# Gathering whole token rows, two expert blocks to a buffer

## The chip, the cores and the metric

The kernel runs on one core of one Trainium2 chip. The metric is device time in microseconds (us) of the whole program, a two-layer model in float32. Four compute engines matter here: TensorE (PE) with its weight-load side (PEld), VectorE (DVE), ScalarE (ACT) and GpSimd (POOL). SyncE (SP) only issues transfers. All transfers, from whichever queue, run on the core's 16 DMA engines.

## The reference

The model is two blocks in a row over 512 tokens of width 1024. The change touches only the routed experts of the first block:

```
N_EXPERTS = 64; TOP_K = 8; D_EXPERT = 256; ROUTED_SCALE = 2.5
h2   = rmsnorm(x) * (1 + scale) + shift                  # [512, 1024]
# each token picks 8 of 64 experts (4 of 8 groups first), weights normalised, times 2.5
for each expert e, over the tokens that chose it:
    hid = silu(h2[tok] @ w_gate[e]) * (h2[tok] @ w_up[e])   # [n, 256]
    out[tok] += weight * (hid @ w_down[e])                  # [n, 1024]
```

Before this stage lie the first block's mixers and projections, after it the second block.

## The kernel before

All work is written out by hand per engine, with semaphores between them; `wait_ge(*x.at("step", i))` waits until step i of engine x is done. Each engine runs its own instruction list in order.

**Blocks.** The 512 x 8 routed pairs are sorted into slots, 64 slots to a block, 96 blocks. Experts are ranked by their token count. The 32 fullest have two blocks each, the other 32 have one, and `blocks` alternates between the two kinds. Slots beyond an expert's count are empty; their index lies out of bounds and the transfer skips them. What does not fit goes to an overflow loop (`ov_*`), which each engine enters before block `MID` = 48 (POOL at 47), at least once.

**The tables.** DVE turns the slot table into `GI`, indices of half rows. A token's 4 KB row of `h2` is stored as two 2 KB halves (`K.h2d2`), and partitions 0 to 63 index the first half, 64 to 127 the second. The scatter of results uses the same `GI`.

**The queue of one block**, i from 0 to 95:

- POOL, `gather(i + 6)` (line 2296): one indirect DMA of 128 half rows into `XG[i % 6]`, one block to a buffer, six buffers. Then it waits for `y(i)` from ACT and for the scatter of block i - 3 (they add into the same of three DRAM tensors `yd`), and issues `scatter(i)` (line 2322), an indirect DMA that adds 128 half rows of results. POOL enters the overflow loop just before `gather(53)`.
- PE, step i: the gate and up products of block i (line 2006, 32 matmul instructions); then `tokens_T(i + 1)` (line 2068), four 128x128 transposes of the next block's gathered rows; then the down product of block i - 1 (line 2020); then the transposition of the hidden rows of block i (line 2027).
- ACT: silu (2097); `y(i - 1)`, the weighted copy of the down product into one of four buffers `Y` (2104), which first waits for the scatter of block i - 5 out of that buffer; the copy of the transposed hidden rows (2107).
- DVE: silu times up (2279); then `tokens_dve(i + 1)` (line 2289), the copy of the transposed tokens out of PSUM into `XGT`, of which there are two, one block each.
- SP: the weights of an expert, 2 MB of gate and up (`in_w_gu`, line 1912) and 1 MB of down (`in_w_dn`, line 1915), into a ring of three, each as soon as its place is freed by the expert three before.

Before the loop, POOL issues gathers 0 to 5 and PE runs `tokens_T(0)`; `tokens_T(1)` also waits for the slot tables.

Of the kernel before, what the change touches and what calls it, by code (L numbers as in the profile page):

```python
# [1825 lines left out]
def experts(K):  # L1826
# [4 lines left out]
    S, C, I, ps = K.S, K.C, K.I, K.ps  # L1831
    H2T = K.H2T
    hi = K.area(K.base1 + 4096, K.keep1)
    XG = [hi(512) for _ in range(4)]
    ar = K.area(K.keep1)
    ar(4096)
    GUB, DNB = [], []
# [8 lines left out]
    OH, TMP = K.area(ar.at - 4096)(2048), ar(2048)  # L1846
    rows = K.area(K.R0, K.R0 + 3072)
    Y = [rows(512) for _ in range(4)]
    XGT = [rows(512).rearrange("p (c n) -> p c n", c=4) for _ in range(2)]
    later = K.area(K.base1)  # L1850
    HD, HDT = [later(128), later(128)], [later(128), later(128)]
    r256 = lambda: ar(256).rearrange("p (t n) -> p t n", t=4)
# [8 lines left out]
    ERK, NOV, EXI = ar(64), ar(1), ar(MORE)  # L1861
    SLf, SLi, Pi, Bi, Pf, Bf = (ar(32) for _ in range(6))
    E0, TB, GI, WS = (later(160) for _ in range(4))
    HS, HST = [Y[0][:, 0:256], Y[0][:, 256:512]], [Y[1][:, 0:256], Y[1][:, 256:512]]
    PSI, PSW = PP[:, :, 0, :], PP[:, :, 1, :]
    XGf = K.area(K.base1 + 4096)(2048)
# [79 lines left out]
    def pe(e):  # L1946
        K.norm2.done(e)
        e.wait_ge(*came_wr.at())
        for t in range(4):
            for k in range(8):  # L1950
                x = e.matmul(ps[5][:, t * 64:t * 64 + 64], H2T[:, k, hs(t)], wrt[:, k, :], start=(k == 0), stop=(k == 7))
        x.then_inc(*mm.up("route"))
        e.wait_ge(*came_gu[2].at(0))
        shared_gu(e, 0)
        shared_gu(e, 1)
        shared_down(e, 0)
        e.wait_ge(*dve.at("sel"))
        for t in range(4):
            for q in range(t):
                e.matmul(ps[6][:, t * 64:t * 64 + 64], C["ones"], SEL[:, q, :], start=(q == 0), stop=False)  # L1960
            x = e.matmul(ps[6][:, t * 64:t * 64 + 64], C["sup"], SEL[:, t, :], start=(t == 0), stop=True)
        for q in range(4):
            e.matmul(ps[7][:, 0:64], C["ones"], SEL[:, q, :], start=(q == 0), stop=(q == 3))
        for q in range(4):
            x = e.matmul(ps[7][0:64, 64:66], SEL[:, q, :], C["ones"][:, 0:2], start=(q == 0), stop=(q == 3))
        x.then_inc(*mm.up("counts"))
        shared_down(e, 1)
        e.wait_ge(*dve.at("H"))
        e.matmul(ps[5][:, 0:64], C["ones"][0:64, :], G1[0:64, :], start=True, stop=True)
        e.matmul(ps[5][0:2, 64:128], C["tok"][0:64, 0:1].broadcast_to([64, 2]), H[0:64, :], start=True, stop=True).then_inc(*mm.up("ranks"))  # L1970
        e.wait_ge(*dve.at("novc"))
        e.matmul(ps[7][:, 128:192], novc.broadcast_to([64, 128]), C["sup"][0:64, 0:64], start=True, stop=True)
        e.matmul(ps[7][:, 192:194], novc.broadcast_to([64, 128]), C["ones"][0:64, 0:2], start=True, stop=True)
        e.matmul(ps[7][0:64, 194:196], C["up"][0:64, 0:64], novc.broadcast_to([64, 2]), start=True, stop=True).then_inc(*mm.up("over"))
        shared_gu(e, 2)
        e.wait_ge(*dve.at("main"))
        e.matmul(ps[5][:, 128:128 + MORE], C["ones"][0:64, :], Z[0:64, 0:MORE], start=True, stop=True).then_inc(*mm.up("whose"))
        shared_hid(e, 2)
        shared_gu(e, 3)
        shared_y(e, 2)  # L1980
        shared_down(e, 3)
        e.wait_ge(*dve.at("POSd"))
        e.wait_ge(*dve.at("PSI"))
        e.wait_ge(*dve.at("exi"))
        e.wait_ge(*pool_.at("PSW"))
        for n in range(32):
            e.wait_ge(*dve.at("BS", n))
            e.matmul(ps[6][:, 0:160], PP[:, n, :, :].rearrange("p u j -> p (u j)"), BS[n % 12], start=(n == 0), stop=(n == 31)).then_inc(*mm.up("table", n))
        e.wait_ge(*dve.at("TB"))
        for u in range(2):  # L1990
            for j in range(2):
                x = e.matmul(ps[7][64 * j:64 * j + 64, u * 160:u * 160 + 160], K.ident[:, 64 * u:64 * u + 64], TB, start=True, stop=True, skip_group_check=True)
        x.then_inc(*mm.up("table2"))
        tokens_T(e, 0)
        for i in range(N + 1):
            if i == MID:
                ov_pe(e)
            if i < N:
                w = blocks[i][0]
                e.wait_ge(*came_gu[place_of(w)].at(w))  # L2000
                e.wait_ge(*dve.at("xt", i))
                if i >= 2:
                    e.wait_ge(*dve.at("hid", i - 2))
                for k in range(8):
                    for j in range(2):
                        x = e.matmul(ps[i % 2][64 * j:64 * j + 64, 0:256], XGT[i % 2][:, k % 4, (k // 4) * 64:(k // 4) * 64 + 64],  # L2006
                                     GUB[place_of(w)][:, k, j * 256:(j + 1) * 256], start=(k == 0), stop=(k == 7), skip_group_check=True)
                x.then_inc(*mm.up("gu", i))
                if i + 1 < N:
                    tokens_T(e, i + 1)  # L2010
            if i > 0:
                q = i - 1
                w = blocks[q][0]
                e.wait_ge(*came_dn[place_of(w)].at(w))
                e.wait_ge(*act_.at("hidT", q))
                if q >= 2:
                    e.wait_ge(*act_.at("y", q - 2))
                for j in range(2):
                    for c in range(2):
                        x = e.matmul(ps[4 + q % 2][64 * c:64 * c + 64, :], HDT[q % 2][:, 64 * j:64 * j + 64],  # L2020
                                     DNB[place_of(w)][:, j, c * 512:(c + 1) * 512], start=(j == 0), stop=(j == 1), skip_group_check=True)
                x.then_inc(*mm.up("dn", q))
            if i < N:
                e.wait_ge(*dve.at("hid", i))
                if i >= 2:
                    e.wait_ge(*act_.at("hidT", i - 2))
                e.transpose(ps[2 + i % 2][:, 0:128], HD[i % 2], K.ident).then_inc(*mm.up("hidT", i))
# [28 lines left out]
        shared_hid(e, n)  # L2056
        shared_y(e, n)

    def tokens_T(e, i):
        e.wait_ge(*came_xg[i % 6].at(i))  # L2060
        if i >= 2:
            e.wait_ge(*dve.at("xt", i - 2))
        p = ps[6 + i % 2]
        if i == 1:
            e.wait_ge(*dve.at("slots"))
            e.wait_ge(*act_.at("ws"))
        for c in range(4):
            x = e.transpose(p[:, hs(c)], XG[i % 6][:, hs(c)], K.ident)
        x.then_inc(*mm.up("xt", i))

    def act(e):
        K.norm2.done(e)
# [36 lines left out]
    def shared_act1(e, n):  # L2109
# [3 lines left out]
            e.wait_ge(*mm.at("s_hidT", n - 2))  # L2113
        p = gu2(ps[n % 2][:, :])
        h = HS[n % 2].rearrange("p (j f) -> p j f", j=2)
        up = XGT[n % 2].rearrange("p c n -> p (c n)")[:, 0:256].rearrange("p (j f) -> p j f", j=2)
        e.activation(h, p[:, :, 0, :], ACT.Silu).then_inc(*act_.up("s_silu", n))
        e.activation(up, p[:, :, 1, :], ACT.Copy).then_inc(*act_.up("s_up", n))

# [71 lines left out]
    def place(e):  # L2191
# [69 lines left out]
        e.tensor_copy(TB, ps[6][:, 0:160]).then_inc(*dve.up("TB"))  # L2261
        e.wait_ge(*mm.at("table2"))
        e.tensor_scalar(E0, ps[7][:, 0:160], 0.0, 8192.0, ALU.is_equal, ALU.mult).then_inc(*dve.up("E0"))
        e.wait_ge(*dve.now())
        e.scalar_tensor_tensor(out=GI.bitcast(I32), in0=ps[7][:, 0:160], scalar=C["below"], in1=E0, op0=ALU.add, op1=ALU.add).then_inc(*dve.up("slots"))

    def dve_(e):
# [4 lines left out]
        weights(e)  # L2272
        place(e)
        tokens_dve(e, 0)
        for i in range(N):
            if i == MID:
                ov_dve(e)
            e.wait_ge(*act_.at("silu", i))
            e.tensor_tensor(HD[i % 2], HD[i % 2], ps[i % 2][:, 128:256], ALU.mult).then_inc(*dve.up("hid", i))  # L2279
            if i + 1 < N:  # L2280
                tokens_dve(e, i + 1)

    def tokens_dve(e, i):
        e.wait_ge(*mm.at("xt", i))
        if i >= 2:
            e.wait_ge(*mm.at("gu", i - 2))
        else:
            e.wait_ge(*pool_.at("s_hid", 3))
        e.tensor_copy(XGT[i % 2], heads(ps[6 + i % 2][:, :])).then_inc(*dve.up("xt", i))

    def gather(e, i):
        if i < N:
            if i >= 6:
                e.wait_ge(*mm.at("xt", i - 6))
            b = blocks[i][1]
            e.indirect_dma_start(XG[i % 6], None, K.h2d2, off(GI.bitcast(U32)[:, b:b + 1]), bounds_check=1023,  # L2296
                                 oob_is_err=False).then_inc(*came_xg[i % 6].up(i))

    def pool(e):
        K.norm2.done(e)  # L2300
        all_of(e, K.came_h2)
        for n in range(4):
            e.wait_ge(*act_.at("s_up", n))
            h, up = HS[n % 2], XGT[n % 2].rearrange("p c n -> p (c n)")[:, 0:256]
            e.tensor_tensor(h, h, up, ALU.mult).then_inc(*pool_.up("s_hid", n))
        e.wait_ge(*dve.at("PSI"))
        e.tensor_tensor(PSW, PSW, per_row(WK, 32, 64), ALU.mult).then_inc(*pool_.up("PSW"))
# [20 lines left out]
    came_ov = S.dma("ovn")  # L2328
    pdump, pdump2 = K.tiny(1), K.tiny(1)
    gcol, wcol = K.tiny(1), K.tiny(1)  # L2330
    XG += [later(512), later(512)]
    xr, yb, hd, hdt = later(512), later(512), later(128), later(128)
    xtr = later(512).rearrange("p (c n) -> p c n", c=4)
    b_gu, b_dn, b_t, b_ht = ps[MID % 2], ps[(MID + 1) % 2], ps[6 + (MID + 1) % 2], ps[2 + MID % 2]
# [1195 lines left out]
```

## Time and profile before

| | us |
|---|---|
| median of 3 runs | 2975.85 |
| lowest and highest of them | 2966.8, 2976.09 |
| the profiled execution | 2970.56 |
| its span, first to last instruction | 2968.2 |
| of it the block loop, first gate/up product to last scatter issue | 1025 to 1675 |
| one step of PE in the loop that waits for nothing | 6.32 |

The profile is of one execution. Busy time is the union of an engine's instructions. The idle time before an instruction is attributed to what released it; a DMA's time to landing runs from its issue to the last of its semaphore increments. Queue q0 holds what POOL issues, q1 what SP issues. A DMA share of 1 means that all 16 engines were moving packets all the time.

### The profile page before, as it was taken

Reading aid. Unit: us, or ns where it says so; the run is one execution under the profiler, and the core shown is the slowest. Engines: PE = TensorE matmul, PEld = TensorE weight load, DVE = VectorE, ACT = ScalarE, POOL = GpSimd, SP = SyncE. Lnnn points to the kernel's source line nnn. Section 1 sums busy time; section 2 is a strip of 40 time slices with the busy share of each in tenths; the row PEclk is TensorE's granted clock in tenths of the full one; section 3 lists DMA queues with packets and bytes.
Section 4 is the critical chain, followed back from the end, with each engine's and each line's share of the span. In section 5 each row is a group of like instructions: output and inputs, shape, how many; then the busy total and the mean of one; then the engine's idle time right before and its main releaser. Section 6 shows DMA issues by size and latency. Waiting matters only on the chain.

```text
span 2968.2 us, 37292 instructions
## 1 busy us (share of the span) xinstructions
PE 2643.1 (89%) x15649; PEld 1311.4 (44%) x15649; DVE 876.0 (30%) x1556; ACT 438.3 (15%) x970; POOL 474.2 (16%) x379
## 2 busy tenths in 40 slices
PE   7998689999999899998999599987988888888886
PEld 4545567754445454454445244642323223322232
DVE  2044556531133511111111369631121112111212
ACT  2012223211022111111111211610000000000001
POOL 0002234412001243343434211010000000000000
PEclk9999899999999999999999799987999999999999
DMA  5110256423224499999999713248999999999997
GB/s 236 57 57 0 90 188 197 154 93 128 85 80 154 183 377 384 378 342 345 372 370 377 262 74 106 107 182 339 425 427 426 425 427 426 425 427 425 427 426 302
DMA packets 107005, 794.45 MB, mean 268 GB/s; under 512 B 20098, under 2 KB 20482, under 8 KB 55384
## 3 DMA queue, kind: packets, MB, share of 16 engines
q1 hardware_dynamic: 81352, 744.03, 61.7%
q0 software_dynamic: 23648, 39.65, 5.4%
q10 hardware_dynamic: 1840, 8.40, 0.7%
q8 instruction: 125, 2.05, 0.3%
q14 instruction: 40, 0.33, 0.0%
HBM read 769.63 MB, written 39.91 MB: 273 GB/s over the span
## 4 chain that ended last, share of the span: by engine, by line
PE 59%; DMA 27%; DVE 9%; issue 3%; ACT 2%; POOL 0%; SPq 0%; POOLq 0%; ACTq 0%; DVEq 0%
DMA arena<-in_w_down 15%; DMA yd<-arena 8%; PE b L3225 8%; PE b L2006 6%; PE b L1565 5%; PE b L579 4%; PE b L2020 3%; PE b L3240 3%; DVE arena L2709 3%; PE b L581 3%; PE b L3265 3%; DMA arena<-h2d,arena 2%; PE b L1632 2%; PE b L1583 2%; DVE arena L3349 1%
## 5 line engine op out<-in xcount | busy, mean ns | idle before, releaser
L3225 PE MATMUL b<-arena 128*64 128x512 f32 x2048 | 453.3, 600 | 25.0 <-DMA arena<-in_w_up 13.4
L2006 PE MATMUL b<-arena 128*64 128x256 f32 x3072 | 358.1, 386 | 5.0 <-DMA arena<-in_w_gu 3.8
L3225 PEld LDWEIGHTS b<-arena 128*64 128x64 f32 x2048 | 156.4, 138 | 316.2 <-issue 274.4
L3240 PE MATMUL b<-arena 128*64 128x512 f32 x1024 | 232.0, 597 | 64.6 <-DMA arena<-in_w_down 49.6
L2006 PEld LDWEIGHTS b<-arena 128*64 128x64 f32 x3072 | 214.2, 137 | 117.9 <-issue 6.7
L2322 POOL DMA_INDIRECT yd<-arena x96 | 152.2, 1585 | 336.6 <-ACT arena L2104 140.4
L2020 PE MATMUL b<-arena 128*64 128x512 f32 x768 | 187.5, 609 | 0.7 <-issue 0.7
L2279 DVE TENSOR_TENSOR arena<-arena,b 128x128 f32<-128x128 f32 x96 | 27.8, 290 | 521.3 <-ACT arena L2097 521.3
L3240 PEld LDWEIGHTS b<-arena 128*64 128x64 f32 x1024 | 72.0, 136 | 223.3 <-issue 116.4
L3363 DVE TENSOR_TENSOR arena<-arena,b 128x512 f32<-128x512 f32 x32 | 20.6, 686 | 475.5 <-PE b L3225 475.5
L1565 PE MATMUL b<-arena 128*128 128x512 f32 x370 | 159.4, 592 | 0.8 <-DVE arena L1387 0.8
L3394 POOL DMA_INDIRECT arena<-h2d,arena x8 | 7.6, 954 | 709.2 <-PE b L3210 679.1
L579 PE MATMUL b<-arena 128*128 128x512 f32 (+1 forms) x320 | 113.1, 515 | 1.4 <-DVE arena L466 1.4
L3265 PE MATMUL b<-arena 64*128 64x512 f32 x256 | 97.6, 649 | 16.6 <-DVE arena L3349 15.8
L3279 ACT ACTIVATE arena<-b 128x512 f32<-128x512 f32 x32 | 17.4, 596 | 642.8 <-PE b L3225 642.8
L2638 PE MATMUL b<-arena 128*128 128x512 f32 x256 | 110.7, 592 | 0.8 <-ACT arena L283 0.8
L1565 PEld LDWEIGHTS b<-arena 128*128 128x128 f32 x370 | 69.9, 189 | 89.6 <-issue 88.6
L2296 POOL DMA_INDIRECT arena<-h2d,arena x96 | 100.1, 1043 | 44.6 <-issue 28.0
L2104 ACT ACTIVATE arena<-b,arena 128x512 f32<-128x512 f32 x96 | 66.3, 690 | 274.6 <-PE b L2020 143.0
L259 POOL TENSOR_TENSOR arena<-arena 128x1024 f32<-128x1024 f32 x14 | 33.2, 2374 | 403.8 <-DVE arena L254 227.2
L3349 DVE TENSOR_TENSOR arena<-arena,b 128x512 f32<-128x512 f32 x128 | 82.1, 686 | 38.7 <-PE b L3265 38.7
L2709 DVE SCALAR_TENSOR_TENSOR arena<-arena 128x512 f32<-128x512 f32 x120 | 90.4, 753 | 4.1
(491 smaller groups left out, 3112.6 us busy)
## 6 DMA issues: line engine op xcount, KB each, us to landing
arena<-in_w_gu SPq DMA_DIRECT2D x65, 2048.0 KB, 12.9
arena<-in_w_down SPq DMA_DIRECT2D x54, 2048.0 KB, 34.2
arena<-in_w_gate SPq DMA_DIRECT2D x48, 2048.0 KB, 38.6
arena<-in_w_up SPq DMA_DIRECT2D x47, 2048.0 KB, 38.8
arena<-in_w_dn SPq DMA_DIRECT2D x65, 1024.0 KB, 10.1
arena<-in_w_mod SPq DMA_DIRECT2D x80, 512.0 KB, 4.3
arena<-in_w_in SPq DMA_DIRECT2D x18, 2048.0 KB, 8.7
arena<-in_w_up SPq DMA_DIRECT2D x34, 1024.0 KB, 36.8
```

What stands on the lines that cost most here:

```text
L579: x = e.matmul(p[:, 0:n], w[:, k, hs(f)], HT[:, k, lo:lo + n], start=(k == 0), stop=(k == 7))
L1565: x = e.matmul(p[:, :], HT[:, k, hs(t)], w[:, at:at + 512], start=(k == 0), stop=(k == 7))
L2006: x = e.matmul(ps[i % 2][64 * j:64 * j + 64, 0:256], XGT[i % 2][:, k % 4, (k // 4) * 64:(k // 4) * 64 + 64], GUB[place_of(w)][:, k, j * 25 ...
L2020: x = e.matmul(ps[4 + q % 2][64 * c:64 * c + 64, :], HDT[q % 2][:, 64 * j:64 * j + 64], DNB[place_of(w)][:, j, c * 512:(c + 1) * 512], sta ...
L2296: e.indirect_dma_start(XG[i % 6], None, K.h2d2, off(GI.bitcast(U32)[:, b:b + 1]), bounds_check=1023, oob_is_err=False).then_inc(*came_xg[i ...
L2322: e.indirect_dma_start(K.yd[i % 3], off(GI.bitcast(U32)[:, b:b + 1]), Y[i % 4], None, bounds_check=1023, oob_is_err=False, compute_op=ALU. ...
L2638: x = e.matmul(p[:, :], w[:, k, hs(where)], HT[:, k, 0:512], start=(k == 0), stop=(k == 7))
L2709: e.scalar_tensor_tensor(out=CY[:, b, :], in0=VC[:, b, k:k + 512], scalar=cw[:, b, k:k + 1], in1=CY[:, b, :], op0=ALU.mult, op1=ALU.add).t ...
L3225: x = e.matmul(ps[b + c][64 * hf:64 * hf + 64, :], XS[:, kb, (n % 2) * 64:(n % 2) * 64 + 64], w[kb % 2][:, u * 512:u * 512 + 512], start=( ...
L3240: x = e.matmul(p[64 * hf:64 * hf + 64, :], H[:, c * 4 + j, hi * 64:hi * 64 + 64], w[i // 2][:, (i % 2) * 1024 + hf * 512:(i % 2) * 1024 + ...
L3265: e.matmul(back_to[n, t, hf][:, :], ST[n % 2][r, hs(t)], Y2[n % 2][r, :], start=True, stop=True).then_inc(*mm.up("back", n, t, hf))
L3349: e.tensor_tensor(o, o, back_to[q, t, hf][:, :], ALU.add).then_inc(*dve.up("add", q, t, hf))
```

## The change

Gathers fetch whole 4 KB token rows, 64 for a block. Even blocks land on partitions 0 to 63, odd ones on 64 to 127 of the same buffer; there are three buffers of a pair. A new index table `GT` (token numbers) is computed by two extra DVE instructions. A pair's rows are transposed in two portions of four 128x128 transposes: portion u takes 512 of the 1024 columns of both blocks of pair u // 2. The portion for step i + 2 is done in step i, and needs both gathers of its pair. DVE copies each portion into one of two pair buffers `XT`; the gate and up products read 64 of its 128 columns. The overflow loop is left on half rows. `gather(g)` waits until the pair three before has been transposed.

```diff
@@ buffers @@
-    XG = [hi(512) for _ in range(4)]
+    XG = [hi(1024) for _ in range(2)]
...
-    XGT = [rows(512).rearrange("p (c n) -> p c n", c=4) for _ in range(2)]
+    UP = [rows(512) for _ in range(2)]
+    pairs = K.area(ar.at - 6144)
+    XT = [pairs(1024).rearrange("p (k n) -> p k n", k=8) for _ in range(2)]
...
+    GT = TB
...
-    XG += [later(512), later(512)]
+    XG.append(later(1024))
@@ PE @@
         tokens_T(e, 0)
+        tokens_T(e, 1)
         for i in range(N + 1):
             if i == MID:
+                e.wait_ge(*dve.at("xt", MID + 1))
                 ov_pe(e)
             if i < N:
                 w = blocks[i][0]
+                r = slice(64 * (i % 2), 64 * (i % 2) + 64)
                 e.wait_ge(*came_gu[place_of(w)].at(w))
-                e.wait_ge(*dve.at("xt", i))
+                e.wait_ge(*dve.at("xt", i // 2 * 2 + 1))
...
-                        x = e.matmul(ps[i % 2][64 * j:64 * j + 64, 0:256], XGT[i % 2][:, k % 4, (k // 4) * 64:(k // 4) * 64 + 64],
+                        x = e.matmul(ps[i % 2][64 * j:64 * j + 64, 0:256], XT[i // 2 % 2][:, k, r],
...
-                if i + 1 < N:
-                    tokens_T(e, i + 1)
+                if i + 2 < N:
+                    tokens_T(e, i + 2)
...
-    def tokens_T(e, i):
-        e.wait_ge(*came_xg[i % 6].at(i))
-        if i >= 2:
-            e.wait_ge(*dve.at("xt", i - 2))
-        p = ps[6 + i % 2]
-        if i == 1:
+    def tokens_T(e, u):
+
+        first = u // 2 * 2
+        for i in (first, first + 1):
+            e.wait_ge(*came_xg[i % 6].at(i))
+        if u >= 2:
+            e.wait_ge(*dve.at("xt", u - 2))
+        if u == 1:
             e.wait_ge(*dve.at("slots"))
             e.wait_ge(*act_.at("ws"))
         for c in range(4):
-            x = e.transpose(p[:, hs(c)], XG[i % 6][:, hs(c)], K.ident)
-        x.then_inc(*mm.up("xt", i))
+            x = e.transpose(ps[6 + u % 2][:, hs(c)], XG[u // 2 % 3][:, hs(4 * (u % 2) + c)], K.ident)
+        x.then_inc(*mm.up("xt", u))
@@ DVE @@
-        e.wait_ge(*dve.now())
+        e.tensor_scalar(TB, ps[7][:, 0:160], 0.5, -0.5, ALU.mult, ALU.add).then_inc(*dve.up("half"))
+        e.wait_ge(*dve.now())
+        e.tensor_tensor(GT.bitcast(I32), TB, E0, ALU.add).then_inc(*dve.up("tokens"))
         e.scalar_tensor_tensor(out=GI.bitcast(I32), in0=ps[7][:, 0:160], scalar=C["below"], in1=E0, op0=ALU.add, op1=ALU.add).then_inc(*dve.up("slots"))
...
         tokens_dve(e, 0)
+        tokens_dve(e, 1)
...
-            if i + 1 < N:
-                tokens_dve(e, i + 1)
-
-    def tokens_dve(e, i):
-        e.wait_ge(*mm.at("xt", i))
-        if i >= 2:
-            e.wait_ge(*mm.at("gu", i - 2))
+            if i + 2 < N:
+                tokens_dve(e, i + 2)
+
+    def tokens_dve(e, u):
+        e.wait_ge(*mm.at("xt", u))
+        if u >= 4:
+            e.wait_ge(*mm.at("gu", u // 2 * 2 - 3))
         else:
             e.wait_ge(*pool_.at("s_hid", 3))
-        e.tensor_copy(XGT[i % 2], heads(ps[6 + i % 2][:, :])).then_inc(*dve.up("xt", i))
+        e.tensor_copy(XT[u // 2 % 2][:, 4 * (u % 2):4 * (u % 2) + 4, :], heads(ps[6 + u % 2][:, :])).then_inc(*dve.up("xt", u))
@@ POOL @@
     def gather(e, i):
         if i < N:
             if i >= 6:
-                e.wait_ge(*mm.at("xt", i - 6))
-            b = blocks[i][1]
-            e.indirect_dma_start(XG[i % 6], None, K.h2d2, off(GI.bitcast(U32)[:, b:b + 1]), bounds_check=1023,
+                e.wait_ge(*mm.at("xt", i // 2 * 2 - 5))
+            b, r = blocks[i][1], slice(64 * (i % 2), 64 * (i % 2) + 64)
+            e.indirect_dma_start(XG[i // 2 % 3][r, :], None, K.h2d, off(GT.bitcast(U32)[0:64, b:b + 1]), bounds_check=511,
                                  oob_is_err=False).then_inc(*came_xg[i % 6].up(i))
```

The remaining lines of the diff put the shared expert's up values into `UP`, whose place `XGT` had.

## Rows read from the trace of the kernel before

**Rows 1.** The page: span, engines' busy time, DMA share in 40 slices.

```profile
span 2968.2 us, 37292 instructions
...
PE 2643.1 (89%) x15649; PEld 1311.4 (44%) x15649; DVE 876.0 (30%) x1556; ACT 438.3 (15%) x970; POOL 474.2 (16%) x379
...
DMA  5110256423224499999999713248999999999997
```

**Rows 2.** Windows: length, engines' busy time (instructions), granted clock, DMA share, GB/s.

```profile
1083.10:1319.50 236.40, 229.62 (x1623) 116.68 (x1622) 34.72 (x72) 40.69 (x108) 91.98 (x70) 0.99 1.02 380
1319.50:1333.50 14.00, 12.64 (x91) 6.44 (x90) 1.94 (x4) 2.37 (x7) 7.20 (x6) 1.00 0.74 204
1333.50:1384.80 51.30, 42.58 (x273) 21.54 (x272) 6.82 (x14) 6.03 (x17) 18.32 (x18) 0.90 0.85 321
1384.80:1637.90 253.10, 247.01 (x1758) 126.11 (x1757) 37.62 (x78) 44.25 (x118) 102.62 (x78) 1.00 1.01 375
```

**Rows 3.** Waits in 1060 to 1660: total us, times, longest.

```profile
ACT arena L2104 <- DMA yd<-arena: 131.6, 30, 7.4
...
PE b L2068 <- DMA arena<-h2d,arena: 14.2, 16, 2.0
...
PE b L2006 <- DMA arena<-in_w_gu: 3.8, 1, 3.8
```

**Rows 4.** Timeline, one step without a wait: start, us, engine, line.

```profile
1048.79 0.66 PE L2068 MATMUL b<-arena 128*128 128x128 f32 x4
...
1051.37 0.69 ACT L2104 ACTIVATE arena<-b,arena 128x512 f32<-128x512 f32 x1 [2.18 <-PE b L2020]
...
1052.85 1.58 POOL L2322 DMA_INDIRECT yd<-arena  x1 [3.38 <-ACT arena L2107]
1054.73 1.04 POOL L2296 DMA_INDIRECT arena<-h2d,arena  x1 [0.30 <-issue]
1055.11 0.42 PEld L2068 LDWEIGHTS b<-arena 128*128 128x128 f32 x4 [0.39 <-issue]
```

**Rows 5.** Line 2296, gathers: windows 1020:1035, 1039:1095, 1098:1320, 1620:1640.

```profile
DMA to landing us min/median/max: 4.0/8.5/9.5
...
DMA to landing us min/median/max: 10.5/13.7/17.5
...
DMA to landing us min/median/max: 12.3/21.5/23.1
...
DMA to landing us min/median/max: 13.1/13.4/13.7
```

**Rows 6.** DMA queues in 1100 to 1600: packets, MB, share of 16 engines.

```profile
q1 hardware_dynamic: 14445, 157.88, 76.9%
q0 software_dynamic: 16574, 25.21, 21.4%
```

**Rows 7.** The same in 1018:1034.5 (six gathers) and 2010:2030 (block 2's).

```profile
q0 software_dynamic: 544, 1.50, 26.7%
...
q0 software_dynamic: 288, 1.05, 18.1%
...
arena<-h2d,arena POOLq DMA_INDIRECT x2, 4.4
```

**Rows 8.** Timeline, the start of the loop.

```profile
1017.26 0.33 DVE L2263 TENSOR_SCALAR arena<-b 128x160 f32<-128x160 f32 x1 [0.87 <-PE b L1992]
...
1022.96 1.12 PE L2068 MATMUL b<-arena 128*128 128x128 f32 x4 [5.75 <-DMA arena<-h2d,arena]
...
1024.11 0.69 DVE L2289 COPY arena<-b 128x512 f32<-128x512 f32 x1 [6.11 <-PE b L2068]
```

**Rows 9.** Timeline around the overflow's end.

```profile
1371.80 1.03 POOL L2296 DMA_INDIRECT arena<-h2d,arena  x1 [0.30 <-issue]
...
1375.49 6.65 PE L2006 MATMUL b<-arena 128*64 128x256 f32 x32 [3.76 <-DMA arena<-in_w_gu]
...
1384.78 3.67 PE L2006 MATMUL b<-arena 128*64 128x256 f32 x32
```

More of the change, by code:

```diff
@@ L2115, in shared_act1 @@
         h = HS[n % 2].rearrange("p (j f) -> p j f", j=2)
-        up = XGT[n % 2].rearrange("p c n -> p (c n)")[:, 0:256].rearrange("p (j f) -> p j f", j=2)
+        up = UP[n % 2][:, 0:256].rearrange("p (j f) -> p j f", j=2)
         e.activation(h, p[:, :, 0, :], ACT.Silu).then_inc(*act_.up("s_silu", n))
@@ L2303, in pool @@
             e.wait_ge(*act_.at("s_up", n))
-            h, up = HS[n % 2], XGT[n % 2].rearrange("p c n -> p (c n)")[:, 0:256]
+            h, up = HS[n % 2], UP[n % 2][:, 0:256]
             e.tensor_tensor(h, h, up, ALU.mult).then_inc(*pool_.up("s_hid", n))
```

## The prediction

> **What bounds the kernel now.** I read the page first: PE is busy 89% of the span and no other compute engine over 30% [rows 1]. The slices of DMA show two stretches at 9 tenths: the block loop of this change and block 2's experts. So in the loop two things are full at once, and the question is which of them gives. The windows say it in numbers [rows 2]. A step of PE is 45 matmul instructions (32 + 4 + 8 + 1). The window from 1083 has 1623 of them, 36 steps in 236.4 us, 6.57 us a step; the one from 1385 has 1758, 39 steps in 253.1 us, 6.49. A step that waits for nothing takes 1055.11 - 1048.79 = 6.32 [rows 4]. The DMA share of both windows is 1.01 to 1.02, so the engines never rest. The waits name where PE loses its 0.2 us a step: on gathered rows at its transposes (14.2 us), hardly on weights (3.8 us) [rows 3].
>
> Why is a gather late? Its landing takes 10.5 to 17.5 us at the loop's start and 21.5 in the median later [rows 5]. The queues explain it [rows 6, 7]. Six gathers made 544 packets with two small transfers among them; 6 x 80 = 480 are 64 data packets and 16 semaphore packets each, so two 2 KB half rows already share a packet. A scatter is 128 + 16. Check: some 73 gathers x 80 + 74 scatters x 144 = 16,496, against 16,574 packets of q0 in 500 us [rows 6]. Per engine a block is then 5 + 9 = 14 packets of q0 and, with 18 packets for an expert's weights and 1.5 blocks to an expert, 12 of q1. A mean packet of q1 takes 0.769 x 16 x 500 / 14,445 = 0.426 us, one of q0 0.214 x 16 x 500 / 16,574 = 0.103. So the DMA work of a block is 12 x 0.426 + 14 x 0.103 = 6.56 us an engine: as much as the step measures, and more than PE's 6.32. Where packets of the two queues alternate, a gather behind its scatter waits 14 x 0.53 = 7.4 us for turns alone. The stage is bound by DMA by a hair, and what DMA can't do shows as q0's queue growing until PE waits. "Arbitration" in the Trainium skill's page DMA: Bandwidth & Descriptors (section on queues) says that each engine alternates between its queues packet by packet; the growth of the landings from 10.5 to 21.5 agrees with it, and it changes no term.
>
> **The change part by part.** *PE's work*: the same 45 instructions of the same shapes a step, 0. *DVE's copies*: the same 512 columns; at even i the products wait for a copy that DVE makes after `hid(i - 1)`, behind PE's down product as before, 0. If that cover went (transposes late), the copy is 0.69 behind 2.3 us of down and hidden transposes, still 0. *The wait ahead of the overflow loop*: a copy of 0.69 issued before the down product, 0. *POOL's descriptor lists*: 64 entries for 128. A list takes 1.04 us now [rows 4]; the saving lies between nothing and all of that, and POOL sits idle 3.4 us in the step, so 0 either way.
>
> *Packets of a gather.* Block 2's gather is of whole 4 KB rows: two of them, 128 rows each, made 288 packets, 2 x (128 + 16) [rows 7]. A row is one packet. So 64 rows are 64 packets and 16 of semaphores: 80, exactly as now, with the same bytes. Bounds: a packet of one piece instead of two could be cheaper by at most all of the 4 x 0.103 = 0.4 us a block, or the half set of partitions could slow it; I take 0, because the packets and bytes are equal. The page SBUF — State Buffer (Terms, port swizzle) says that 64 partitions reach only half of the ports that 128 do, which speaks against this change. No row here has a 64-partition transfer; if the rule bites, the price is that of the second rival below.
>
> *The start.* DVE gets two more instructions before POOL may gather, 0.33 each like L2263 [rows 8]: +0.65. The first transposes need gathers 0 and 1, not 0 alone. They share one queue: gather 0 took 4.0, the fourth 9.5 [rows 5], issued 1.34 apart (1.04 + 0.30 [rows 4]), so they land (9.5 - 4.0) / 3 + 1.34 = 3.2 apart: +3.2. Portion 1's transposes (1.12 on the cold clock) now precede block 0: +1.1, and 0.65 comes back at the end, where step 94 has none. Sum +4.3, between 2 and 7.
>
> *The overflow.* POOL issues gather 53 only when its overflow pass is over, at 1371.80 [rows 9]. Now PE needs block 53's rows in step 51, which is late anyway because its weights arrive at 1375.49, and in the 6.65 us of cold products that follow the gather lands unseen. After the change portion 52 needs both 52 and 53 in step 50, whose products end near 1369.0. One gather of 5 packets stands ahead and it has 5 of its own: 10 x 0.53, on top of the floor of 4.0, is 9.3, landing at 1381.1. From there 2.7 (transposes, down, hidden transposes: 6.32 less 3.6 for the products) to block 51, 6.3 for that step and 3.0 for the cold clock (6.65 against 3.67): block 52 begins at 1393.1, not 1384.78. That is +8.3; with landings of 4.0 and 12.3 it is +3 and +11.3.
>
> *The lookahead*, the main term. Gather g is issued in POOL's iteration g - 6, which comes 1054.73 - 1048.79 = 5.94 us after PE's transposes of that step [rows 4]. Now it is needed at the transposes of step g - 1: 5 x 6.32 - 5.94 = 25.7 us may pass. After the change the odd block of a pair is needed two steps sooner: 3 x 6.32 - 5.94 = 13.0 us (19.3 for the even one). Nearly every landing of the long stretches is over that [rows 5]. What happens then is a closed loop: over two pairs, 4 steps, PE takes at least 6.32 + 5.94 + L = 12.3 + L, with L the landing. With L held at 21.5 a step would be 8.4. But L is a queue, not a constant: at a step of 8.4 the engines have 6.56 us of work, 78%, and no queue would stand. L falls until loop and DMA agree. Where DMA had just caught up it was 13.1 to 13.7, in the first steps 10.5 and up [rows 5]. At L = 14.1 the loop gives 26.4 / 4 = 6.6 a step, just above DMA's 6.56. So I take 6.6 against the present mean of 489.5 / 75 = 6.53: 75 x 0.07 = +5.3, and the 10 steps that now run at 6.32 while the queue builds up lose some 0.15 each, +1.5. Sum +7. PE's floor bounds it below (6.32: -16), and L = 15.5 above (6.95: +36).
>
> Sum: 4.3 + 8.3 + 7 = +19.6 on the profiled execution's 2970.56, so 2990. The median of the runs is 5.3 higher than that execution; I put the forecast between the two readings, at 2993.
>
> **The rivals.** *The queue does not shrink* (0.10). The weights are issued as places come free and may keep q1 full even at a slower step, so that q0 goes on getting one turn in two. For it: landings reached 17.5 while PE still ran at 6.32 [rows 5]. Against it: the 78% above. With L = 17.5 the loop gives 7.45, + 0.92 x 85 = +78, with the rest some 3062.
>
> *The half set of partitions is slower* (0.10). If a 64-row gather is carried by 8 engines, those have 9 packets for it, not 5: 4 x 0.53 = +2.1 on L, 16.2 in place of 14.1, 7.1 a step, +43 more, 3035. It decides once L is up by 1 us or so. Against it: nothing in the rows shows an engine's share; both halves take turns, so the mean load stays.
>
> *No change that a median can tell* (0.24). DMA sets 6.53 to 6.56 before and after, the queue is merely shorter, and the overflow's gather lands in 5 us: 4.3 + 3 = +7, 2980 on the same scale.
>
> *Faster* (0.10). A packet of one whole row is cheaper than one of two halves. DMA's 6.56 then falls under PE's 6.32, and all that PE waits for gathers is gone. It decides from 0.24 us a block and engine, over half of what a gather's packets take. The long stretches would run at 6.33, 75 x 0.2 = -15; with the start's +2 and the overflow's +3 that is -10, on the scale of the forecast 2963. Against it: q0's packets count the same, and block 2's rows show no shorter transfer.
>
> **How the numbers follow.** The case of the sum has 0.46; with L from 13.7 to 15 (6.5 to 6.83 a step) its own range is 2985 to 3012. About 0.3% (9 us) is what a measurement of this kernel can tell from no change, its three runs lying 9.3 us apart. Slower: 0.46 + 0.10 + 0.10 = 0.66; same: 0.24; faster: 0.10. The range from 2967 to 3038 leaves out the first rival and the faster case.
>
> **What the changed kernel's profile would show.** Gathers' landings of 13 to 15 us in the median, not 21; the wait of y for a scatter (131.6 us now [rows 3]) nearly gone, since the tighter loop holds fewer transfers in the queue; PE's waits at line 2068's transposes at even steps alone, 0.3 to 1.5 us each and more than 14.2 us in sum; packets of q0 unchanged; one wait of about 12 us for block 53 behind the overflow. The forecast is wrong if the landings stay at 20 (then 3060 and more), or if a step stays at 6.5 and the overflow costs nothing.

## The result, and the profile after

The changed kernel takes 3030.30 us (median of 4 runs, 3026.05 to 3035.52), against 2975.97 before (2966.8 to 2977.74): a ratio of 1.0188, interval 1.0171 to 1.0205. The forecast was slower, 2993 with 2967 to 3038: the sign was right, the size a third of what came. The time lies inside the range, near its top, but the range reached up there for longer landings of the gathers, and it is not those that came; that it holds the result is luck.

The windows of the changed kernel (length, busy time and instructions of PE, PEld, DVE, ACT, POOL, granted clock, DMA share, GB/s). They run from block 1's gate and up products to block 47's, on to block 52's, and on to block 91's:

```profile
1043.80:1374.90 331.10, 300.81 (x2071) 150.79 (x2070) 44.69 (x93) 51.72 (x138) 115.73 (x91) 0.96 0.98 332
1374.90:1432.90 58.00, 41.91 (x271) 20.79 (x270) 6.84 (x14) 5.94 (x17) 17.30 (x17) 0.85 0.85 312
1432.90:1700.30 267.40, 250.09 (x1758) 126.89 (x1757) 37.67 (x78) 44.29 (x118) 99.28 (x78) 0.99 1.00 348
```

The first window of before, from its block 1 to its block 47; the other two are in [rows 2]:

```profile
1032.50:1333.50 301.00, 292.81 (x2070) 149.44 (x2070) 44.34 (x92) 51.46 (x137) 119.70 (x92) 0.99 0.99 364
```

The same 46 and 39 steps (2071 and 1758 instructions by 45) take 331.1 and 267.4 us instead of 301.0 and 253.1: 7.20 and 6.86 us a step instead of 6.54 and 6.49. The DMA share is still 0.98 to 1.00, but at 332 and 348 GB/s instead of 364 and 375. The engines are as full as before and bring less. That is the row to stop at: late gathers alone do not lower what full engines bring (e2 below, with late gathers and old packets, has 360 and 372 GB/s at shares of 0.98 and 1.01).

The DMA queues of the changed kernel in 1100 to 1600 (packets, MB, share of 16 engines), to be held against [rows 6]:

```profile
q1 hardware_dynamic: 13172, 143.47, 76.2%
q0 software_dynamic: 15309, 23.98, 21.3%
```

A mean packet of q1 took 0.762 x 8000 / 13,172 = 0.463 us (8000 are 500 us of 16 engines), where it had taken 0.426; one of q0 0.213 x 8000 / 15,309 = 0.111 for 0.103. The counts per block are the same (the page has 23,648 packets on q0 in both kernels). So a block's DMA work is 12 x 0.463 + 14 x 0.111 = 7.11 us, not 6.56.

The means hide which packets grew. The trace's packet records, sorted by size, tell it (mean ns of one in 1100 to 1600; e5, e6 and e8 are explained below):

| packet | before | after | e6 | e5 | e8 |
|---|---|---|---|---|---|
| weights, 16 KB | 624 | 666 | 671 | 627 | 632 |
| weights, 8 KB | 330 | 374 | 360 | 332 | 340 |
| gathered rows, 4 KB | 166 | 193 | 191 | 163 | 170 |
| scattered half rows, 2 KB | 181 | 180 | 180 | 182 | 182 |

Of these only packets that write into the core's own memory became longer; those of the scatter, which write to DRAM, did not. And it is a part of them that did: nine in ten of the 16 KB packets took up to 625 ns before and up to 785 after, while the median moved from 611 to 625.

The timeline of the changed kernel around one wait (start, us, engine, line):

```profile
1107.72 0.98 POOL L2307 DMA_INDIRECT arena<-h2d,arena  x1 [0.30 <-issue]
...
1126.25 1.08 PE L2076 MATMUL b<-arena 128*128 128x128 f32 x4 [5.45 <-issue]
1127.27 3.16 PE L2026 MATMUL b<-arena 128*64 128x512 f32 x8
```

The first row is gather 15, the second portion 14, which needs it: at most 18.5 us to landing, against 13.0 that the new lookahead leaves, and PE stands 5.45 us. The landings themselves are not recorded in this profile, so it names no releaser ("issue"); that the wait is for the gather follows from the program, whose other condition there, DVE's copy of portion 12, was met two steps earlier.

PE had run without a pause before this wait, and the down products behind it take 3.16 us and not 1.94. The two windows, with the granted clock third from the end:

```profile
1104.00:1120.00 16.00, 16.00 (x121) 8.52 (x121) 1.92 (x4) 3.12 (x8) 6.62 (x5) 1.00 1.04 366
1126.20:1131.00 4.80, 4.75 (x17) 1.93 (x19) 0.69 (x1) 0.52 (x1) 0.00 (x0) 0.63 0.98 363
```

The clock fell from full to 0.63, mostly the lower of its two levels, after 5.45 us of standing, and over the whole first window it is 0.96 instead of 0.99.

Where the profiled spans' 60.1 us (3028.3 less 2968.2) lie; the medians are 54.3 us apart:

| stretch | before | after | difference | forecast |
|---|---|---|---|---|
| up to gather 0's issue | 1018.9 | 1022.7 | +3.8 | +0.65 |
| from there to block 1's products | 13.6 | 21.1 | +7.5 | +4.3 |
| blocks 1 to 47 and 52 to 91 | 554.1 | 598.5 | +44.4 | +7 |
| blocks 47 to 52, with the overflow | 51.3 | 58.0 | +6.7 | +8.3 |
| block 91 to the end | 1330.3 | 1328.0 | -2.3 | -0.65 |

One term is off by 37 us. The rest is near its forecast.

### The profile page after: what moved, and what is told of

It reads as the page before. It is cut to its first block, busy times and chain, and to the rows that moved or that the text cites. A ratio compares the mean times of both kernels' runs of the same rounds, so it can differ in the third digit from the quotient of the medians.

```text
span 3028.3 us, 37297 instructions
## 1 busy us (share of the span) xinstructions
PE 2660.3 (88%) x15649; PEld 1317.3 (43%) x15649; DVE 876.7 (29%) x1558; ACT 438.1 (14%) x970; POOL 466.3 (15%) x379
## 3 DMA queue, kind: packets, MB, share of 16 engines
q0 software_dynamic: 23648, 39.64, 5.6%
## 4 chain that ended last, share of the span: by engine, by line
PE 68%; DMA 17%; DVE 9%; issue 4%; ACT 1%; POOL 0%; SPq 0%; ACTq 0%; DVEq 0%; POOLq 0%
DMA arena<-in_w_down 15%; PE b L2012 11%; PE b L3236 7%; PE b L2026 6%; PE b L1565 5%; PE b L579 4%; PE b L3251 3%; DVE arena L2720 3%; PE b L581 3%; PE b L3276 3%; PE b L2076 2%; PE b L1632 2%; PE b L1583 2%; PE b L722 1%; DVE arena L3360 1%
## 5 line engine op out<-in xcount | busy, mean ns | idle before, releaser
L3236 PE MATMUL b<-arena 128*64 128x512 f32 x2048 | 452.1, 599 | 24.5 <-DMA arena<-in_w_up 12.5
L3251 PE MATMUL b<-arena 128*64 128x512 f32 x1024 | 233.2, 600 | 61.5 <-DMA arena<-in_w_down 45.7
L2026 PE MATMUL b<-arena 128*64 128x512 f32 x768 | 198.0, 638 | 0.7 <-issue 0.7
L2076 PE MATMUL b<-arena 128*128 128x128 f32 x384 | 64.2, 292 | 72.1 <-issue 58.2
L3405 POOL DMA_INDIRECT arena<-h2d,arena x8 | 7.6, 953 | 709.7 <-PE b L3221 679.6
L2307 POOL DMA_INDIRECT arena<-h2d,arena x96 | 93.9, 979 | 45.1 <-issue 27.1
```

The lines of the kernel that those rows point to most:

```text
L2076: x = e.transpose(ps[6 + u % 2][:, hs(c)], XG[u // 2 % 3][:, hs(4 * (u % 2) + c)], K.ident)
L2307: e.indirect_dma_start(XG[i // 2 % 3][r, :], None, K.h2d, off(GT.bitcast(U32)[0:64, b:b + 1]), bounds_check=511, oob_is_err=False).then_in ...
L3236: x = e.matmul(ps[b + c][64 * hf:64 * hf + 64, :], XS[:, kb, (n % 2) * 64:(n % 2) * 64 + 64], w[kb % 2][:, u * 512:u * 512 + 512], start=( ...
L3251: x = e.matmul(p[64 * hf:64 * hf + 64, :], H[:, c * 4 + j, hi * 64:hi * 64 + 64], w[i // 2][:, (i % 2) * 1024 + hf * 512:(i % 2) * 1024 + ...
```

## The experiments

**Theory A** is the prediction's: only the shorter lookahead costs, and what is off is how far the queue shrinks. **Theory B**: gathers that write one half of the partitions make other packets longer too, whatever the lookahead. Means of a q1 packet are worked out as above, from each run's own row for 1100 to 1600. "Ahead" is how long the last gather that a step needs may take to land. The ratios are of medians of several runs, each against runs of the kernel before made with it; packets, steps and stretches are of one profiled execution each.

| run | rows land on | ahead, us | ratio to before (95%) | q1 packet, us | us a step, two stretches | 47 to 52, us |
|---|---|---|---|---|---|---|
| before | all, 128 halves | 25.7 | 1 | 0.426 | 6.54, 6.49 | 51.3 |
| after | one half, 64 | 13.0 | 1.0188 (1.0171 to 1.0205) | 0.463 | 7.20, 6.86 | 58.0 |
| e1 | one half, 64 | 25.7 | 1.0167 (1.0130 to 1.0204) | 0.458 | 6.94, 6.97 | 51.7 |
| e2 | all, 128 halves | 13.0 | 1.0060 (1.0042 to 1.0077) | 0.432 | 6.64, 6.43 | 62.1 |
| e3 | all, 128 a pair | 13.0 | 1.0055 (1.0036 to 1.0073) | 0.432 | 6.67, 6.45 | 60.0 |
| e4 | all, 128 a pair | 25.7 | 1.0022 (1.0005 to 1.0040) | 0.428 | 6.58, 6.58 | 47.8 |
| e5 | 32 to 95, 64 | 25.7 | 1.0065 (1.0043 to 1.0087) | 0.428 | 6.54, 6.62 | 52.7 |
| e6 | 0 to 63, 64 | 25.7 | 1.0195 (1.0171 to 1.0219) | 0.460 | 7.05, 6.87 | 55.4 |
| e7 | all, 128 halves | 38.3 | 1.0005 (0.9988 to 1.0021) | 0.426 | 6.53, 6.55 | 48.9 |
| e8 | 32 to 95, 64 | 13.0 | 1.0069 (1.0047 to 1.0092) | 0.433 | 6.67, 6.59 | 58.6 |
| e9 | one half, 64 | 13.0 | 1.0201 (1.0172 to 1.0230) | 0.467 | 7.23, 6.96 | 58.6 |

### e1: the long lookahead given back

```diff
     XG.append(later(1024))
+    XG.append(K.area(K.R0 + 2048, K.R0 + 3072)(1024))
...
-        for i in range(6):
+        e.wait_ge(*pool_.at("s_hid", 3))
+        for i in range(8):
             gather(e, i)
...
-            gather(e, i + 6)
+            gather(e, i + 8)
```

The rest of the edit counts buffers and semaphores by four pairs. The added wait is for POOL's own last instruction before the gathers, which ends 16 us before DVE releases gather 0; it costs nothing.

> The changed kernel with a fourth pair buffer and gathers eight blocks ahead, so that the odd block of a pair may take 5 steps less 5.94 us = 25.7 us to land, as before the change, in place of 13.0; the 64-row gathers stay. Theory A (the shorter lookahead alone costs the time, L is the queue's): the loop goes back to 6.5 us a step and the overflow wait goes, 2970 to 2985. Theory B (gathers into half the partitions slow all packets: in the changed kernel a mean packet of the weights' queue took 0.762 x 16 x 500 / 13,172 = 0.463 us against 0.426 before): the DMA work of a block stays at 12 x 0.463 + 14 x 0.111 = 7.1 us, the step at 6.9 to 7.1, 3010 to 3030, with GB/s of the loop near 350. Both: 2990 to 3005.

3023.42 us. The wait behind the overflow is gone, and still a step takes 6.94 us and the packets 0.458. Its windows, for blocks 1 to 47 and 52 to 91:

```profile
1050.20:1369.50 319.30, 300.17 (x2073) 151.18 (x2072) 44.37 (x93) 51.26 (x138) 116.87 (x92) 0.96 1.00 343
...
1421.20:1693.20 272.00, 255.22 (x1758) 129.07 (x1757) 37.46 (x78) 43.81 (x118) 97.72 (x77) 0.96 1.01 354
```

319.3 + 272.0 is 37.2 us more than the 554.1 of before, with before's lookahead: a full DMA at a lower rate. Theory A can't give that. What the lookahead still adds on top does not show in the whole: the ratios of e1 and the changed kernel, 1.0167 and 1.0188, have intervals that overlap.

### e2: the kernel before, with the short lookahead

```diff
-        for i in range(6):
+        for i in range(4):
             gather(e, i)
...
-            gather(e, i + 6)
+            gather(e, i + 4)
```

> The kernel before (128 half rows, all partitions) with its gathers issued four blocks ahead in place of six: a gather may take 3 x 6.32 - 5.94 = 13.0 us, what the changed kernel gives its odd blocks. Theory A: as slow as the changed kernel, 3015 to 3040, since each gather is bound and not only every second. Theory B: the queue shrinks as the prediction had it, 6.6 to 6.7 us a step, 2985 to 3000, with the weights' mean packet at 0.42 to 0.43 us.

2990.58 us, inside the range of theory B and far from that of theory A. That it is also the prediction's sum (2990 to 2993) is in part luck: that sum holds 4.3 us for a start that this kernel does not have, and its other two terms came out differently, as follows. The issues of this run in 1100 to 1600 (count, median us to landing):

```profile
arena<-h2d,arena POOLq DMA_INDIRECT x72, 12.5
```

The median landing is 12.5 us; with the long lookahead it is 21.5 [rows 5], or 21.0 in this window. The queue does shrink to what the loop allows, and the two stretches together cost 305.5 + 250.9 - 554.1 = +2.3 us. The overflow's stretch costs +10.8, more than in the changed kernel, perhaps since here every gather has the short lookahead and not each second.

### e3 and e4: one gather of 128 whole rows for a pair

```diff
-            e.indirect_dma_start(XG[i // 2 % 3][r, :], None, K.h2d, off(GT.bitcast(U32)[0:64, b:b + 1]), bounds_check=511,
+            e.indirect_dma_start(XG[p % 3], None, K.h2d, off(PI.bitcast(U32)[:, p:p + 1]), bounds_check=511,
...
-            gather(e, i + 6)
+            if i % 2:
+                gather(e, i // 2 + 3)
```

These are the lines of e3; e4 has 4 in place of 3, and e1's fourth buffer. `PI` is a new table, made by DVE: a pair's 64 + 64 token numbers in one column of 128 partitions.

> The changed kernel with one gather of 128 whole rows for a pair, issued where the pair's second gather was (three buffers, the same lookahead of 13.0 us): all 128 partitions at once, 144 packets for 160, one descriptor list for two. Theory A: no change but for the packet less per engine, 3015 to 3030. Theory B: packets at 0.43 us again, 2985 to 3005.

> One gather of 128 whole rows for a pair and a fourth pair buffer, so 25.7 us of lookahead. Both theories: the time of before or a little under, 2955 to 2980, since two packets in 28 of the gathers' and scatters' queue go away per pair and engine and the wait behind the overflow (some 7 us) is gone; if it stays over 2990, the cause is in the pairs themselves (the start, or the order of the transposes).

e3 takes 2988.05 us, e4 2976.14. Whole rows and pairs are all but harmless once all partitions are written at once; e3 differs from the changed kernel by little else (one list and 144 packets a pair for two lists and 160), and is 40 us faster. What is left of the change, 0.55%, is what the prediction summed up for it (2993 on 2976 is 0.58%); in e3's profile 2.4 us lie in the start, 4.3 in the long stretches and 8.7 around the overflow, where the forecast had 4.3, 7 and 8.3. Its queue q1:

```profile
q1 hardware_dynamic: 14088, 153.72, 76.1%
```

That is 0.432 us a packet. The fourth buffer in e4 takes away the wait behind the overflow (47.8 us), and e4's ratio is 1.0022 (up to 1.0040), at best equal to before and not under it: the packet less per gather bought nothing that shows. Nor is a packet of one whole row cheaper than one of two halves: with all partitions written its mean is 165 and 161 ns in e3 and e4, against 168 and 161 in e2 and e7.

### e5, e6 and e8: only the partitions that the rows land on

```diff
+    XH = [K.area(ar.at - 4096 + 1024 * n)(1024) for n in range(4)]
...
-            b, r = blocks[i][1], slice(64 * (i % 2), 64 * (i % 2) + 64)
-            e.indirect_dma_start(XG[i // 2 % 4][r, :], None, K.h2d, off(GT.bitcast(U32)[0:64, b:b + 1]), bounds_check=511,
+            b, r = blocks[i][1], slice(32, 96)
+            e.indirect_dma_start((XG, XH)[i % 2][i // 2 % 4][r, :], None, K.h2d, off(GT.bitcast(U32)[0:64, b:b + 1]), bounds_check=511,
```

This is e5 against e1; e6 has `slice(0, 64)`. e8 is the e5 edit made to the changed kernel itself, with three buffers of each kind. All three leave the odd blocks' rows out of the computation, and in e5 and e8 half of an even block's rows stand where the odd block is read. The work and the transfers stay; from block 91 to the end these kernels take 1327.8 to 1329.1 us, before 1330.3.

> The kernel of e1 (64-row gathers, four pair buffers), but every gather writes partitions 32 to 95, the odd blocks' into buffers of their own that nothing reads; so the odd blocks' rows are left out of the computation, while transfers, packets, descriptor order and all engines' instructions stay. It tells two readings of theory B apart. Ports (partitions 0 to 63 and 64 to 127 each reach half of the ports into the memory, 32 to 95 both halves): the weights' packets return to 0.43 us, the loop to 6.5 to 6.6 a step, 2970 to 2990. Engines (a list of 64 rows loads some DMA engines more, wherever it lands): packets and time as e1, 3010 to 3025.

> The same, but every gather writes partitions 0 to 63 (the odd blocks' again into buffers that nothing reads). Ports: one half now carries all gathers and not each half in turn, so at least as slow as e1, 3025 to 3050, with packets of 0.46 us or more. Engines: as e1 and as e5, 3010 to 3025.

> The changed kernel itself (three pair buffers, the short lookahead, 64-row gathers), only that every gather writes partitions 32 to 95, the odd blocks' into buffers that nothing reads, so the odd blocks' rows are left out. It completes the square with e1 and e5. If the half set of partitions and the lookahead are two separate costs: the packets as before the change (0.43 us), stretches at 6.5 to 6.65 us a step, the wait behind the overflow still there, 2988 to 3000. If a 64-row gather needs the long lookahead to be harmless, over 3005.

e5 takes 2992.26 us, e6 3027.51, e8 2989.64. e5's time is 2 us over the range expected by the ports; its packets and, within 0.02 us, its steps came as expected, and the times of e6 and e8 lie inside their ranges. The q1 rows of e5, of e6 and of e8:

```profile
q1 hardware_dynamic: 14363, 156.72, 76.8%
```

```profile
q1 hardware_dynamic: 13423, 146.54, 77.1%
```

```profile
q1 hardware_dynamic: 13908, 151.70, 75.2%
```

0.428 us a packet in e5, 0.460 in e6 and 0.433 in e8. e5 and e6 have the same lists of 64 rows, the same packets and the same instructions; only the target rows differ. The same holds between e8 and the changed kernel: 0.433 and 0.463 us, 1.0069 and 1.0188. So of the change's 1.9%, 1.2% goes with the place of landing. So what costs is that a 64-row gather lies wholly in partitions 0 to 63 or 64 to 127, and not that it has 64 rows, and not the loading of DMA engines by the order of the list, which is the same in all. e6 is no slower a step than e1 (7.05, 6.87 against 6.94, 6.97), so taking both halves in turn spares nothing. Its windows, for the same two stretches:

```profile
1041.40:1365.90 324.50, 299.50 (x2073) 151.56 (x2072) 44.55 (x93) 51.10 (x138) 114.22 (x90) 0.97 0.99 337
...
1421.30:1689.30 268.00, 251.65 (x1758) 127.68 (x1759) 37.55 (x78) 43.45 (x117) 95.72 (x75) 0.98 1.01 358
```

No view shows which engine carries a packet, so the place of landing might also choose the engines. But in e6 every gather lands on the same half; if half of the engines carried them all, the others should stand idle in part, and the share is 0.99 and 1.01. Longer packets explain both the full share and the lower GB/s.

The Trainium skill's page SBUF — State Buffer (Door 1: the DMA port swizzle) says that partitions 0 to 63 reach only the 8 even ports of 16, and 64 to 127 the odd ones. By its table of ports and partitions 32 to 95 reach all 16. The runs agree with this in all three placements, in that the cost comes and goes with them; no run sees a port itself, and why packets beside the gathers wait is not shown.

e5 is still 0.65% over before. Of its profile's 22.4 us over, 11.0 lie ahead of gather 0, where kernels that are the same up to there differ as much ("Open", in the section on the prediction), 6.5 in the start (20.1 us from gather 0's issue to block 1, against 13.6) and 5.0 in the second stretch. The first pair waits for two lists, and e4, with one list, is 4 us quicker there (15.8). In this pair the lookahead does not show in the whole: e8 with the short one is at 1.0069, e5 with the long one at 1.0065.

### e7: before, eight ahead

```diff
-            e.indirect_dma_start(XG[i % 6], None, K.h2d2, off(GI.bitcast(U32)[:, b:b + 1]), bounds_check=1023,
+            e.indirect_dma_start(XG[i % 8], None, K.h2d2, off(GI.bitcast(U32)[:, b:b + 1]), bounds_check=1023,
...
-            gather(e, i + 6)
+            gather(e, i + 8)
```

> The kernel before with eight buffers and gathers eight blocks ahead. If DMA's work of 6.56 us a block is the bound, the deeper lookahead only lengthens the queue: landings stay above 20 us, 6.5 us a step, 2965 to 2980, but for the wait at the overflow. If the lookahead of six was itself the limit (PE's waits of 20 us at the transposes), 2950 to 2962.

2976.15 us, no change. Of the waits of this run, the costliest for a DMA (total us, times, longest):

```profile
ACT arena L2105 <- DMA yd<-arena: 203.8, 40, 7.6
```

The wait moves from PE's transposes to the results' buffers, whose scatters ACT awaits (131.6 before [rows 3]), and PE's idle time now lies ahead of its down products (16.7 us); the steps stay at 6.53 and 6.55, with a DMA share of 1.00 and 1.01. So DMA's 6.56 us a block bound the loop before the change, not the number of gather buffers.

### e9: the start

```diff
@@ SP @@
+        e.wait_ge(*came_xg[1].at(1))
         for n, w in enumerate(order):
```

> The changed kernel, with the loading of the third expert's weights held back until gathers 0 and 1 have landed. In the changed kernel the first transposes come 11.7 us after gather 0's issue, against 4.1 before. If the first pair waits because its packets alternate with the weights that start 1.1 us after it, the first transposes come 5 to 7 us after gather 0's issue, and the rest of the loop is as in the changed kernel, total 3020 to 3030; if the 64-row gather itself is slow, they still come after 10 us or more.

The timeline of this run:

```profile
1018.01 1.09 POOL L2308 DMA_INDIRECT arena<-h2d,arena  x1 [16.13 <-DVE arena L2276]
...
1023.35 1.94 PE L2077 MATMUL b<-arena 128*128 128x128 f32 x8 [7.48 <-DMA arena<-h2d,arena]
1023.94 0.35 SPq L1915 DMA_DIRECT2D arena<-in_w_gu  x1
```

The first transposes come 5.3 us after gather 0's issue, not 11.6 (11.7 in the expectation): without the weights' packets between them, two gathers land in 5.3 us. The whole gains nothing that shows (3031.3 us, 2 runs, a microsecond over the range).

## Why the prediction was right and wrong

- **The bound** was read rightly: DMA's work a block, 6.56 us, above PE's 6.32. e7 shows it from the other side.
- **The step that failed** is "Packets of a gather": "I take 0, because the packets and bytes are equal". They are equal, and yet the gathered packets became longer (166 to 193 ns), and with them the weights', whose mean grew by 9% (0.426 to 0.463 us). As the stage is bound by the sum of these packets, this went straight into the step: 7.11 - 6.56 = 0.55 us by 85 steps would be 47 us, and e1 has 37.2 us of it with the long lookahead. The only bound set there, 0.4 us a block, is what a cheaper gather packet could save; for the half set of partitions none was set but the rival's. Most of the price, 12 x 0.037 = 0.44 us a block, is paid by the 12 weight packets beside the gathers.
- **The second rival** named this half set of partitions, with 0.10 and 3035 us, but by a wrong mechanism: eight engines with nine packets each, hence later landings of gathers whose neighbours stay as they are. Landings of 21.5 + 2.1 us still fit into e1's lookahead of 25.7, and yet e1 is 1.7% slower than before; what grew is the weights' packets. e5 and e8 keep 64-row lists and lose the cost, so it is the place of landing. That its 3035 us came near 3030 is luck. The Trainium skill's page SBUF — State Buffer (Terms, port swizzle), which spoke against the change, was set aside because no row showed a 64-partition transfer. A missing row was no reason for 0: the gathers are 16.8 MB beside 201 MB of weights, but the loop had no DMA time to spare.
- **The lookahead** came out as worked out in its mechanism, a landing that shrinks until loop and DMA agree, and smaller in size: +7 forecast, +2.3 in e2 and +4.3 in e3 (306.9 + 251.5 - 554.1). L was taken as 14.1 and is 12.5 in e2 and 13.1 in e3, in the median of 1100 to 1600. The first rival, a queue that does not shrink, is refuted by the same numbers. Between the profiles of e1 and of the changed kernel the short lookahead adds 7.2 us to the two stretches, where one gather took up to 18.5 us; that longer packets make it dearer is likely and not shown.
- **The overflow**: +8.3 forecast, +6.7 measured, 8.7 in e3. In the changed kernel PE stands 10.7 us there (12.1 by the forecast's times), and e1 (+0.4) and e4 (-3.5), with four buffers, lose it.
- **The start**: 4.3 forecast, 7.5 and the 0.65 of DVE measured. Missing was that the weights issued 1.1 us after gather 0 put their packets between those of gathers 0 and 1; e9 takes 6.3 us off that wait by holding them back.
- **What the profile would show**: packets of q0 unchanged and the one wait of some 12 us held. The wait of y for a scatter went away: no such row is left in the changed kernel, and each y starts within 0.1 us of the end of its down product. PE's waits at the transposes are at even steps alone, as forecast, but were put at 0.3 to 1.5 us each and are up to 5.45. The gathers' median landing can't be read there.
- **Open**: what in the chip makes the neighbours' packets longer; why e1's packets are a little shorter than those of the changed kernel (0.458, 0.463); and why e5 keeps 5 us in its second stretch. None was tried further. The 3 us of difference ahead of gather 0 are not the change's: that issue lies between 1018.0 and 1031.1 in the profiles of these kernels, which do the same work ahead of the tables: 1018.9 in the kernel before, 1029.6 and 1031.1 in e2 and e7, which are that kernel up to gather 0.

## What to carry to other kernels

Where DMA's share is 1, an edit to one small transfer has to be priced by what it does to all the others: hold GB/s and the mean packet of every queue before and after, not only counts and bytes. Here the cure was to give the gather all partitions (e3, e4); 64 rows on a range across the middle, 32 to 95, were harmless to the packets too (e5, e8). Two blocks of 64 go into one gather of 128. And a queue's landing time is no constant: when the lookahead was cut by half the median landing fell from 21.0 us to 12.5, and the two long stretches lost 2.3 us and the stretch around the overflow 10.8.

## What the runs showed of the hardware

- 64-row gathers, 512 x 8 rows of 4 KB or 16.8 MB of a loop whose weights alone are 201 MB, made the weights' packets 8 to 9% longer when they landed on partitions 0 to 63 or 64 to 127 (0.458 to 0.463 us, against 0.426 before), and hardly on 32 to 95 (0.428 to 0.433, as with 128 partitions: 0.426 to 0.432).
- Packets into the core's own memory grew (16 KB ones from 624 to 666 ns, 4 KB ones from 166 to 193), packets of the accumulating scatter to DRAM did not (181 and 180 ns).
- An indirect list of 64 rows took POOL 0.98 us and one of 128 half rows 1.04, and one of 128 whole rows 1.07 in e3: the length of the list hardly counts.
